# Weight transfers in pairs from expert 8 on in place of expert 10, and the ninth weight buffer for four pieces in place of six

## The chip, the cores and the metric

One core of one Trainium2 chip runs the whole kernel. The metric is the time of one execution on the device in microseconds; the median of three runs of the kernel before is 1223.11 us (1222.31 to 1225.02).

## The reference, cut to what matters

One decoder layer on 256 prompt tokens and 64 sample tokens. First come the norm, an input projection, two kinds of recurrent heads (HGRN2 and RWKV-7) and an output projection. Then comes a mixture of 32 experts, and each token goes to 4 of them. Nothing of the change touches the first part.

```
logits = h @ w_router + b_router
top_val, top_idx = lax.top_k(logits, TOP_K)            # 4 of 32
gates = softmax(top_val)
# for each expert e and its tokens x:
gu = x @ w_gate_up[e] + b_gate_up[e]                   # (n, 1024) @ (1024, 2048)
gate, up = min(gu[:, :D_FF], 7), clip(gu[:, D_FF:], -7, 7)
y  = ((up + 1) * gate * sigmoid(1.702 * gate)) @ w_down[e] + b_down[e]   # (n, 1024) @ (1024, 1024)
out = x_resid + sum over the 4 experts of gate * y
```

All is 32-bit floating point. An expert has 8 MB of gate and up weights and 4 MB of down weights, 12 MB together and 384 MB for all 32.

## The kernel before, in words

The weights of the experts are cut into pieces of 2 MB (128 partitions of 16 KB, `PIECE` = 4096 elements). `weight_pieces` lists them in order of transfer as `PIECES`: the four up pieces of expert 0, then for every expert e from 1 the four up pieces of e and the two down pieces of e - 1, and the last two down pieces. There are 192. The index of a piece in this list is called k here: the up pieces of expert e are k = 6e - 2 to 6e + 1, and the down pieces of expert e are k = 6e + 8 and 6e + 9 (190 and 191 for expert 31).

A piece lives in one of nine places in SBUF. Places 0 to 7 (`wslot`) are taken in turn; place 8, the ninth, is the tile `spare_slot` and is used by the pieces in `ONCE` alone. `piece_slots` works out for each piece its place (`SLOT`) and the piece that was in that place before (`HELD`). A piece may be sent only when TensorE is done with the piece that its place held: `load_piece` (L647) waits for the semaphore `w_used`, which TensorE raises by one after the last matmul on each piece, and then issues the transfer through the helper `load` (L578) on the queue of SyncE. SyncE does this in order of k for all pieces from `FIRST` = 9 on (L687), so a piece whose place is not free holds up all pieces behind it. Nothing else goes through SyncE's queue in this stage, except for one small load at expert 29.

Pieces in `WIDE` are sent in pairs: places 0/1, 2/3, 4/5 and 6/7 lie side by side in SBUF (`wpair`), and one transfer of 4 MB (128 partitions of 32 KB) fills both. It waits for the piece that the second of the two places held, `HELD[k + 1]`. `WIDE` begins at the up pieces of expert 10, k = 58, and ends before those of expert 30, k = 178. From expert `EW` = 8 on the up weights are laid out in rows so that two pieces lie side by side in DRAM too.

TensorE takes the pieces in the same order. `arrived` (L1573) waits until the transfer of a piece has landed. An expert is 8 chunks of up matmuls (`up_chunk`, L1585, two chunks a piece), then the first down piece of the expert before (`down_part`, L1619), eight transposes of this expert's gate and up rows (L1610), and the second down piece. Among the up chunks stand the gather of the tokens of a later expert (L1560), and in every second expert the turning of the slots (L1647) and the scatter of finished rows into the output (L1656). VectorE and ScalarE compute the gated product and add the scattered rows.

Of the kernel before, what the change touches and what calls it, by code (L numbers as in the profile page):

```python
# [38 lines left out]
NE, TOPK, DFF = 32, 4, 1024  # L39
# [211 lines left out]
PIECES = weight_pieces()  # L251
PLACE = {x: k for k, x in enumerate(PIECES)}
EW = 8
WIDE = range(PLACE["up", EW + 2, 0], PLACE["up", NE - 2, 0])


ONCE = (8, 17, 26, 35, 44, 53)
FIRST = 9


def piece_slots():

    slot, before, had, n = [], [], {}, 0
    for k in range(len(PIECES)):
        if k in ONCE:
            s = NWS
# [12 lines left out]
def piece_counts():  # L279

    out, n = [], [0] * (NWS + 1)
    for k in range(len(PIECES)):
        s = SLOT[k]
        if k in WIDE and k % 2:
            out.append(out[-1])
# [25 lines left out]
def build(nc, A, O):  # L311
    ctx = ExitStack()
    with ctx:
# [5 lines left out]
        def S(name):  # L319

            if name not in sems:
                sems[name] = ctx.enter_context(nc.semaphore(name))
            return sems[name]
# [76 lines left out]
        def U(stage, k):  # L400

            return DONE[stage, k - 1]
# [173 lines left out]
        def _(sync):  # L576
# [70 lines left out]
            def load_piece(k):  # L647

                kind, e, j = PIECES[k]
                if k in WIDE:  # L650
                    if k % 2 == 0:
                        sync.wait_ge(S("w_used"), HELD[k + 1] + 1)
                        load(wpair[SLOT[k] // 2], rows_in(kind, e, j, 2), f"w{SLOT[k]}_in")
                    return
                slot_ = wslot[SLOT[k]]
                if k == FIRST:
                    for x in range(2):
                        sync.wait_ge(S("unit_filled"), len(UNITS) + 1 + x)
                        load(slot_[:, 1024 * x:1024 * x + 1024], rows_in(kind, e, j)[:, 1024 * x:1024 * x + 1024], ("w0_in", "mid_in")[x])
                    sync.wait_ge(S("w_used"), 1)  # L660
                    load(slot_[:, 2048:PIECE], rows_in(kind, e, j)[:, 2048:PIECE], "end_in")
                    return
                if HELD[k] is not None:
                    sync.wait_ge(S("w_used"), HELD[k] + 1)
                if k >= len(PIECES) - 4:
                    load(slot_[:, 0:PIECE // 2], rows_in(kind, e, j)[:, 0:PIECE // 2], f"w{SLOT[k]}_in")
                    load(slot_[:, PIECE // 2:PIECE], rows_in(kind, e, j)[:, PIECE // 2:PIECE], ("mid_in", "end_in")[j] if e == NE - 1 else ("x0_wo0_in", "x1_wo1_in")[j])
                else:
                    load(slot_, rows_in(kind, e, j), f"w{SLOT[k]}_in")
# [5 lines left out]
            sync.wait_ge(S("unit_filled"), U("var", 3))  # L675
            load_piece(ONCE[0])
            sync.wait_ge(S("mix_rw"), 3)
# [2384 lines left out]
```

## Time and profile before

| | before |
|---|---|
| median of 3 runs | 1223.11 us (1222.31 to 1225.02) |
| the profiled execution | 1221.51 us, of which the span is 1219.4 us |
| PE (matmul) busy | 1192.9 us (98% of the span) |
| VectorE busy | 447.1 us (37%) |
| ScalarE busy | 259.9 us (21%) |
| read from HBM | 430.01 MB |
| chain of the end, by engine | PE 84%, DMA 14%, VectorE 1% |

The span is the time from the first to the last record of the execution; the time of the runs holds some 2 us beside it. PE's clock was granted in full (0.997 of 2.4 GHz on the mean). The experts' stage runs from about 297 us to the end. Each slice of the page's second part is 1219.4 / 40 = 30.5 us long. SPq is SyncE's queue, on which the transfers are issued. A landing is the moment at which the semaphore of a transfer has its full count, and the page's sixth part and the DMA view give the median of the times from issue to landing.

### The profile page before, as it was taken

What the parts mean: (1) busy time and instruction counts of PE and PEld (TensorE: products, weight loads), DVE (VectorE), ACT (ScalarE), POOL (GpSimd) and SP (SyncE); (2) the same over time, 40 slices, a digit from 0 to 9 for tenths busy, and PEclk for the clock granted to TensorE, in tenths of its full rate; (3) what the DMA queues carried; (4) which work ended last, traced back from release to release, by engine and by line L of the source; (5) the groups of instructions that cost most, each with busy time, mean ns of one, the idle gap of its engine ahead of it and who ended that gap; (6) DMA issues with size and microseconds to landing.
All of it is one profiled execution on the core that took longest, in us unless ns stands there. A gap on an engine that the chain in (4) does not pass through costs nothing.

```text
span 1219.4 us, 18273 instructions
## 1 busy us (share of the span) xinstructions
PE 1192.9 (98%) x7824; PEld 575.6 (47%) x7824; DVE 447.1 (37%) x966; ACT 259.9 (21%) x636; POOL 42.8 (4%) x101
## 2 busy tenths in 40 slices
PE   8999999999999999999999999999999999999996
PEld 6777777745443444444443444444443434443332
DVE  3367766754323332333232232323322323222324
ACT  3114434522220211111120112111111111111213
POOL 8000110100000000000000000000000000000000
PEclk9999999999999999999999999999999999999998
DMA  9732202498999999999999999999999999999996
GB/s 286 180 105 70 79 4 72 141 394 331 426 428 427 405 428 429 427 432 426 430 430 429 431 429 430 431 433 431 430 429 431 430 429 429 432 433 426 425 423 225
DMA packets 48940, 436.11 MB, mean 358 GB/s; under 512 B 11461, under 2 KB 26888, under 8 KB 31450
## 3 DMA queue, kind: packets, MB, share of 16 engines
q1 hardware_dynamic: 47812, 431.87, 85.7%
q0 software_dynamic: 960, 3.02, 0.8%
q8 instruction: 64, 1.05, 0.4%
q14 instruction: 18, 0.15, 0.0%
q10 hardware_dynamic: 86, 0.02, 0.0%
HBM read 430.01 MB, written 4.89 MB: 357 GB/s over the span
## 4 chain that ended last, share of the span: by engine, by line
PE 84%; DMA 14%; DVE 1%; ACT 0%; issue 0%; SPq 0%; DVEq 0%; ACTq 0%
PE bank L1585 30%; PE bank L1619 15%; PE bank L890 10%; DMA ring<-in_w_gate_up 9%; PE bank L1560 7%; PE bank L1656 4%; PE bank L1357 3%; DMA ring<-in_w_down 3%; PE bank L1610 2%; DMA mix<-in_w_gate_up 2%; PE bank L1647 1%; PE bank L1109 1%; PE bank L877 1%; PE bank L923 1%; PE bank L1086 1%; DMA hx<-in_state_shift 0%
## 5 line engine op out<-in xcount | busy, mean ns | idle before, releaser
L1585 PE MATMUL bank<-ring,mix 128*64 128x512 f32 x1504 | 344.0, 598 | 5.3 <-DMA ring<-in_w_gate_up 5.2
L1585 PEld LDWEIGHTS bank<-ring,mix 128*64 128x64 f32 x1504 | 101.6, 136 | 204.1 <-issue 198.2
L1619 PE MATMUL bank<-ring,mix 128*64 128x512 f32 x736 | 168.2, 598 | 0.9 <-DMA ring<-in_w_down 0.8
L2903 DVE TENSOR_TENSOR hTb<-bank,w2a 128x512 f32<-128x512 f32 x32 | 22.1, 691 | 368.5 <-PE bank L1610 368.5
L890 PE MATMUL bank<-hTb,ring 128*128 128x328 f32 (+1 forms) x416 | 121.9, 443 | 1.0 <-DVE hTb L2357 0.4
L2153 ACT ACTIVATE mix<-bank,nf 128x256 f32<-128x256 f32 x64 | 26.8, 470 | 449.4 <-PE bank L1560 449.4
L1585 PE MATMUL bank<-mix 128*64 128x512 f32 x496 | 111.4, 595 | 2.8 <-DMA mix<-in_w_gate_up 2.7
L2956 DVE TENSOR_TENSOR mix<-mix,bank 128x512 f32<-128x512 f32 x70 | 48.2, 689 | 158.4 <-PE bank L1656 158.4
L890 PEld LDWEIGHTS bank<-hTb,ring 128*128 128x128 f32 x416 | 76.4, 190 | 33.9 <-issue 2.3
L1619 PEld LDWEIGHTS bank<-ring,mix 128*64 128x64 f32 x736 | 49.6, 136 | 90.0 <-issue 84.0
L1585 PEld LDWEIGHTS bank<-mix 128*64 128x64 f32 x496 | 35.3, 137 | 72.0 <-issue 69.7
L1560 PE MATMUL bank<-mix,hx 128*128 128x256 f32 x240 | 66.1, 418 | 0.0
L2924 DVE SCALAR_TENSOR_TENSOR y_low<-bank,gc,y_high 64x512 fp32r<-64x512 f32 x62 | 46.5, 750 | 49.6 <-ACT y_high L2228 49.1
L1560 PEld LDWEIGHTS bank<-mix,hx 128*128 128x128 f32 x240 | 55.5, 300 | 9.1 <-issue 8.4
L2228 ACT ACTIVATE y_high<-bank,gc 64x512 fp32r<-64x512 f32 x62 | 42.3, 682 | 76.1 <-DVE gc L2938 40.2
L1619 PE MATMUL bank<-mix 128*64 128x512 f32 x240 | 54.8, 598 | 0.0
L1656 PEld LDWEIGHTS bank<-y_high,slot_rows 128*128 128x128 f32 (+1 forms) x96 | 16.2, 186 | 62.5 <-issue 62.5
L2218 ACT ACTIVATE bank<-hTb 128x512 f32<-128x512 f32 x32 | 19.2, 601 | 111.5 <-DVE hTb L2905 111.5
L1656 PE MATMUL bank<-y_high,slot_rows 128*128 128x512 f32 (+1 forms) x96 | 42.3, 480 | 0.0
L2207 ACT COPY g2w<-bank 128x512 f32<-128x512 f32 x32 | 18.7, 585 | 90.8 <-PE bank L1585 90.8
L1560 PEld LDWEIGHTS bank<-raw,hx 64*128 64x128 f32 x112 | 26.9, 303 | 22.9 <-issue 22.7
L1357 PE MATMUL bank<-ring,mix 128*128 128x512 f32 (+1 forms) x96 | 36.9, 600 | 0.0
(445 smaller groups left out, 1132.7 us busy)
## 6 DMA issues: line engine op xcount, KB each, us to landing
ring<-in_w_gate_up SPq DMA_DIRECT2D x30, 4096.0 KB, 24.9
ring<-in_w_gate_up SPq DMA_DIRECT2D x34, 2048.0 KB, 16.1
ring<-in_w_down SPq DMA_DIRECT2D x15, 4096.0 KB, 27.6
mix<-in_w_gate_up SPq DMA_DIRECT2D x10, 4096.0 KB, 25.2
ring<-in_w_down SPq DMA_DIRECT2D x13, 2048.0 KB, 16.3
mix<-in_w_gate_up SPq DMA_DIRECT2D x11, 2048.0 KB, 15.3
mix<-in_w_down SPq DMA_DIRECT2D x5, 4096.0 KB, 28.3
ring<-in_w_in SPq DMA_DIRECT2D x14, 1024.0 KB, 5.6
```

Source lines behind the costliest of these rows:

```text
L890: last_ = mm(b_[:, 0:nn], slot(chunk)[:, c, P * k:P * k + P], hT[:, c, 0:nn], start=(c == 0), stop=(c == KT - 1))
L1357: last_ = mm(o_, lhs_, wo[c_ // 4][:, c_ % 4, 512 * h_:512 * h_ + 512], start=(c_ == 0), stop=(c_ == KT - 1))
L1560: last_ = mm(o, rows_of(tile_, c, r), sel[tile_][0:TN[tile_], :], start=(first and tile_ == TORD[0]), stop=(tile_ == TORD[2]), skip_group_ ...
L1585: last_ = mm(b_[64 * half:64 * half + 64, :].rearrange("s (p q) -> s p q", q=4), toks, cols[:, half], start=(c == 0), stop=(c == KT - 1))
L1610: last_ = nc.tensor.transpose(b_[:, P * q:P * q + P], src[:, q:NCOL:4], ident[:, :])
L1619: last_ = mm(b_[r:r + 64, :], lhs, w[:, o:o + NCOL], start=(j == 0 and q == 0), stop=(j == 1 and q == 3))
L1656: last_ = mm(o[:, :], scatr[r[g], g, P * tile_:P * tile_ + P], y_[r[g], g, :], start=(y_ is yhir and g == half), stop=(stop and y_ is ylor ...
L2153: ins = a(xg[n // 4 % 2][:, 256 * c:256 * c + 256], b[:, 256 * x:256 * x + 256], ACT.Copy, scale=nf2[int(n // 4 >= EW // 4)][:, c:c + 1])
L2228: ins = a(yhir[r, k, :], banks[2][r, :], ACT.Copy, scale=gc[r, g:g + 1])
L2903: v.tensor_tensor(halves(gg), halves(banks[3][:, :]), bias(e, 0), ALU.add).then_inc(S("g1"), 1)
L2924: ins = v.scalar_tensor_tensor(out=ylor[r, k, :], in0=banks[2][r, :], scalar=gc[r, g:g + 1], in1=yhif[r, k, :], op0=ALU.mult, op1=ALU.subt ...
L2956: ins = v.tensor_tensor(o, o, b[:, :], ALU.add)
```

## The change

Two constants change. `WIDE` begins at the up pieces of expert `EW` = 8, k = 46, in place of `EW` + 2 = 10, k = 58. `ONCE` loses its last two pieces, 44 and 53. Pieces 44 and 53 then take places 0 and 1 of the rotation, and the places of all pieces from 44 on move: by one step for 44 to 52 and by two from 53 on.

```
-WIDE = range(PLACE["up", EW + 2, 0], PLACE["up", NE - 2, 0])
-ONCE = (8, 17, 26, 35, 44, 53)
+WIDE = range(PLACE["up", EW, 0], PLACE["up", NE - 2, 0])
+ONCE = (8, 17, 26, 35)
```

The piece of which TensorE must be done before k is sent, worked out by `piece_slots` and `load_piece`:

| k | 44 | 45 | 46 | 47 | 48 | 49 | 50 | 51 | 52 | 53 | 54 | 55 | 56 | 57 | 58/59 | 60/61 | 62/63 | 64/65 |
|---|---|---|---|---|---|---|---|---|---|---|---|---|---|---|---|---|---|---|
| before | 35 | 36 | 37 | 38 | 39 | 40 | 41 | 42 | 43 | 44 | 45 | 46 | 47 | 48 | 50 | 52 | 55 | 57 |
| after | 36 | 37 | 39 (46/47) | | 41 (48/49) | | 43 (50/51) | | 45 (52/53) | | 47 (54/55) | | 49 (56/57) | | 51 | 53 | 55 | 57 |

## Rows read from the trace of the kernel before

**Rows 1.** The page's second part: GB/s moved by the DMA engines in 40 slices.

```profile
GB/s 286 180 105 70 79 4 72 141 394 331 426 428 427 405 428 429 427 432 426 430 430 429 431 429 430 431 433 431 430 429 431 430 429 429 432 433 426 425 423 225
```

**Rows 2.** PE's waits, 889 to 1219 us: waited for, total us, times, longest.

```profile
PE bank L1585 <- DMA ring<-in_w_gate_up: 5.2, 7, 1.3
PE bank L1585 <- DMA mix<-in_w_gate_up: 2.7, 3, 1.3
...
PE bank L1619 <- DMA ring<-in_w_down: 0.8, 2, 0.4
```

**Rows 3.** The chain of the end, in order: start, us, step.

```profile
477.80 3.58 PE bank L1619 x16
...
703.40 3.58 PE bank L1619 x16
...
865.93 24.42 DMA ring<-in_w_gate_up
...
1165.12 33.98 DMA ring<-in_w_down
```

**Rows 4.** Windows: length, busy us by engine, PE clock, DMA share, GB/s.

```profile
411.00:500.00 89.00, 89.00 (x398) 35.88 (x400) 25.39 (x54) 12.92 (x30) 0.00 (x0) 1.00 1.01 428
...
575.00:580.00 5.00, 5.00 (x26) 1.72 (x24) 1.50 (x2) 0.28 (x1) 0.00 (x0) 1.00 0.87 374
...
600.00:1100.00 500.00, 494.11 (x2180) 208.70 (x2178) 145.57 (x321) 79.28 (x203) 0.00 (x0) 1.00 1.00 431
```

**Rows 5.** SyncE's timeline: start, us, transfer issued (k = 45, 46, 48/49, 50, 52, 54, 56, 62, 64).

```profile
471.01 0.33 SPq L578 DMA_DIRECT2D ring<-in_w_down  x1
474.44 0.33 SPq L578 DMA_DIRECT2D ring<-in_w_gate_up  x1
...
486.17 3.77 SPq L578 DMA_DIRECT2D ring<-in_w_gate_up  x2
...
494.32 0.33 SPq L578 DMA_DIRECT2D ring<-in_w_down  x1
...
504.44 0.33 SPq L578 DMA_DIRECT2D mix<-in_w_gate_up  x1
...
517.11 0.33 SPq L578 DMA_DIRECT2D ring<-in_w_gate_up  x1
...
527.53 0.33 SPq L578 DMA_DIRECT2D ring<-in_w_down  x1
...
560.84 0.33 SPq L578 DMA_DIRECT2D ring<-in_w_down  x1
...
573.51 0.33 SPq L578 DMA_DIRECT2D ring<-in_w_gate_up  x1
```

**Rows 6.** PE's timeline: start, us, matmuls merged (k = 47-49, 51, 53, 66).

```profile
525.55 8.80 PE L1585 MATMUL bank<-ring,mix 128*64 128x512 f32 x40
...
538.88 3.65 PE L1619 MATMUL bank<-mix 128*64 128x512 f32 x16
...
548.74 1.94 PE L1585 MATMUL bank<-spare_slot,mix 128*64 128x512 f32 x8
...
607.67 0.65 PE L1585 MATMUL bank<-ring,mix 128*64 128x512 f32 x2
```

**Rows 7.** DMA view, issues at 399.97, 404.71, 471.01, 560.84, 573.51 us, b_down's: KB, us to landing.

```profile
ring<-in_w_gate_up SPq DMA_DIRECT2D x1, 2048.0 KB, 8.7
...
ring<-in_w_gate_up SPq DMA_DIRECT2D x1, 2048.0 KB, 9.4
...
ring<-in_w_down SPq DMA_DIRECT2D x1, 2048.0 KB, 17.6
...
ring<-in_w_down SPq DMA_DIRECT2D x1, 4096.0 KB, 15.7
...
ring<-in_w_gate_up SPq DMA_DIRECT2D x1, 4096.0 KB, 13.4
...
hx<-in_b_down SPq DMA_DIRECT2D x1, 128.0 KB, 2.2
```

## Prediction

> **What bounds the kernel now.** I read the slices of the whole span first. From about 305 us to 1180 us two things are full at once: PE is busy nine tenths and more (the PE line of the same table), and the DMA engines move 425 to 433 GB/s in nearly every slice [rows 1]. So I asked which of the two is late. The waits of PE say it: that view of 270 to 830 us, and of 600 to 889 us, has no row with a transfer; from 889 us to the end it waits 8.7 us for them (5.2 + 2.7 + 0.8, in twelve waits) [rows 2]. The chain of the end agrees: its long DMA links begin at 865.93 us, and the last, ending in the final experts' down weights, lasts 33.98 us, up to 1199.1 us; behind it stand only the last matmuls, the scatter, the norm and the output [rows 3].
>
> The reason lies in two rates. PE alone needs 56.4 us for two experts: the first down matmul of an expert starts at 477.80 us, and that of the expert eight later at 703.40 us, so (703.40 - 477.80) / 4 = 56.4 [rows 3]. Two experts are 12 pieces of 2 MB, 25.17 MB, and at 431 GB/s [rows 4] they need 58.4 us. PE gains 2 us per two experts on the transfers; early on it lives on what lies ready in the buffers, and when that is used up it runs at the pace of the transfers. From there every microsecond that the stream of transfers has lost anywhere is a microsecond at the end. The question is thus only: how late does the stream run behind expert 11, where both versions have the same waits again?
>
> **What the change does to the sum.** I count pieces k in order of transfer; the up pieces of expert e are k = 6e-2 to 6e+1, then come the two down pieces of expert e-1. Up to k = 43 nothing changes. Then three things do.
>
> (1) Pieces 46 to 57 go as six transfers of 4 MB in place of twelve of 2 MB. The SyncE queue gets six DMA instructions and six waits less, of 0.33 us each [rows 5]; that queue waits for buffers most of the time, so this is worth nothing. The rate rises from 428 to 431 GB/s [rows 4]: two pieces take 9.80 us as two transfers and 9.73 us as one. Gain 6 x 0.07 = 0.4 us.
>
> (2) A pair can be issued only when both of its places are free, so it waits for its second place.
>
> (3) Pieces 44 and 53 don't use the ninth buffer any more. So, by (2) and (3), every piece or pair from 44 to 61 waits for PE to be done with a piece one or two later than before (the table of the change has them). (The waits of k = 62 and up are the same before and after: 55, 57, 59 and so on.)
>
> (2) and (3) cost nothing as long as the queue of transfers holds enough. To see whether it does, the time at which PE releases each piece is read from the issues of before, because SyncE issues a piece right when its place is released: piece 36 was released at 471.01 (issue of 45), 37 at 474.44 (of 46), 39 at 486.17 (issue of 48), 41 at 494.32 (50), 43 at 504.44 (52), 45 at 517.11 (54), 47 at 527.53 (56), 55 at 560.84 (62), 57 at 573.51 (64) [rows 5]. The others come from the matmuls that end: 49 at 534.2 (after 525.55 + 8.80), 51 at 542.4 (538.88 + 3.65), 53 at 550.6 (548.74 + 1.94) [rows 6].
>
> Next, how late may an issue be? The one 4 MB transfer of before that met a nearly empty queue is k = 64. It was issued at 573.51 and landed 13.4 us later, at 586.9, while its predecessor, issued at 560.84, landed 15.7 us later, at 576.5 [rows 7]: 10.4 us apart in place of 9.73, so the stream lost 0.7 us. The windows show the hole: 374 GB/s from 575 to 580 us where the mean is 431 [rows 4]. So I take: landing = the later of (previous landing + 9.73) and (issue + 13.4). An issue must come 3.7 us ahead of the previous landing. Two 2 MB transfers that met a short queue (issued at 399.97 and 404.71 us) took 8.7 and 9.4 us [rows 7] where the data alone take 4.9: 3.8 and 4.5 us, near the same.
>
> The steps, from piece 45, which landed at 471.01 + 17.6 = 488.6 [rows 7]. Pieces 44 and 45 are issued 3.4 us later than before and still land on time: 474.44 + 8.7 = 483.1 is ahead of 488.6. Then:
> 46/47: issue 486.17, so 499.6 and not 498.3 (1.3 lost);
> 48/49: issue 494.32, lands 509.3; 50/51: issue 504.44, lands 519.0 (nothing lost);
> 52/53: issue 517.11, so 530.5 and not 528.8 (1.7 lost);
> 54/55: issue 527.53, so 540.9 and not 540.2 (0.7 lost);
> 56/57: 534.2, lands 550.7; 58/59: 542.4, lands 560.4; 60/61: 550.6, lands 570.1; 62/63: 560.84, lands 579.8;
> 64/65: issue 573.51, lands 589.6: the hole of before is gone, since the previous transfer now ends later.
> Before, 64/65 landed at 586.9. The stream is 2.7 us late there: lost 3.7, won back 0.4 by the rate and 0.7 at the old hole (the rest is rounding).
>
> Is PE held up earlier, which would move the releases that I used? No: PE reads 49 only in the 8.80 us behind 525.55 [rows 6], so 46 to 48 not much ahead of that, and they land at 499.6 and 509.3; the smallest reserve near the change is that of 66, which PE reads at 607.67 us [rows 6], and which landed at 586.9 + 9.7 = 596.6 before and lands at 599.3 now. So PE runs as before for a while, with 2.7 us less in store, and meets the pace of the transfers one to two pairs of experts sooner (2.7 / 2 = 1.3). Behind that all is shifted by 2.7 us. At the very end nothing swallows it, since PE waits for the last down weights until 1199.1 us [rows 3] and then has only its own work and the rest of them.
>
> **Sum.** Profiled execution: span 1219.4 us, 1221.51 us with what lies around it. Plus 2.7 gives 1224.2 for that execution. The median of the runs is 1.6 us above it, 1223.11; so the forecast is 1223.11 + 2.7 = 1225.8 us.
>
> **The page and the row.** What the trace shows is 13.4 us from issue to landing with an almost empty queue [rows 7]. The Trainium skill, DMA: Bandwidth & Descriptors, "Anatomy of one DMA", gives a fixed cost of about 2.0 us and a time of 2.0 us + bytes / 436 GB/s, fitted on GpSimd's path; for 4 MB that is an estimate of 11.6 us. By it the needed lead is 1.9 us, and only 52/53 would be late. The row differs by 1.8 us, and I go by the row; the other result is rival B. The same page's rules advise coalescing many small transfers into one large one, which would speak for the change; here the rate rows of both sizes stand at 428 and 431 GB/s, so that is worth 0.4 us.
>
> **The rivals.**
> A, the forecast: +2.7 us, 1225.8.
> B, not slower: the stream loses less than k = 64's landing suggests. The 128 KB load of the down bias, which has 0.3 us of data, landed 2.2 us after its issue [rows 7], so an issue costs as little as 1.9 us beside its data. With landing = issue + 9.73 + 1.9 = issue + 11.6, 52/53 lands at 528.7 and not 527.5, 54/55 at 539.1 and 64/65 at 587.8: +0.9 us, 1224.0. If even that doesn't occur (engines that finish at different times take up the last microsecond), the change keeps only the better rate and the closed hole: -0.4 - 0.7 = -1.1 us, 1222.0. It decides at a lead of 1.9 us in place of 3.7. For it speaks that k = 64 had a lead of 3.0 us (576.5 - 573.51) and yet the DMA share only fell to 0.87 for 5 us [rows 4]; against it stand the two 2 MB loads with 3.8 and 4.5 us.
> C, more: the overhead of the 9.4 us landing (4.5 us) holds for pairs too: issue + 14.2. Then 46/47 lands at 500.4, 52/53 at 531.3, 54/55 at 541.7, and 64/65 at 590.4: +3.5 us, 1226.6.
> D, PE hides it: if the end were set by PE, the result would be 0, 1223.1. Against it stand the DMA waits from 889 us on and the last link of the chain [rows 2, 3].
> E, the shorter queue starves the stream again and again behind expert 11. Against it: the same waits as before hold there, and a stream that is later makes the queue fuller at each issue.
>
> **How the numbers follow.** Chances: A 0.45, B 0.25 (0.9 and -1.1 about alike), C 0.17, D 0.08, E 0.05. A measurement of this kernel tells about 0.2% from no change, 2.45 us. A's 2.7 us stands right at that mark: I give it 0.27 slower and 0.18 same. C and E count as slower (0.20 of 0.22), D and nearly all of B as same. Slower 0.48, same 0.47, faster 0.05. The range goes from the closed-hole case with some scatter of a median (1222.4) to C with some scatter (1227.6).
>
> **What would show it.** Right: the two-piece transfers of k = 46, 52 and 54 land about 13.4 us after their issue, with holes in the DMA rate near 488, 519 and 529 us; no hole near 575; PE has no new wait before 600 us; its first DMA wait comes between 770 and 860 us and not at 890; the sum of these waits grows by about 2.7 us from 8.7. Wrong: holes absent (B), pieces landing 14 us or more after issue (C), a PE wait between 480 and 700 us (then releases move too), or DMA landings that are late while the end isn't (D).

## The result and the profile after

The changed kernel takes 1226.22 us (median of 14 runs, 1224.41 to 1228.12), the kernel before 1223.14 us in its 14 runs. The ratio is 1.0024, with a 95% interval of 1.0017 to 1.0031, which is +2.1 to +3.8 us. The forecast was +2.7 us. The profiled execution of the changed kernel took 1225.37 us with a span of 1223.2 us, 0.9 us below its median. Its span is 3.8 us longer than that of the profiled execution of before.

The windows of the changed kernel show where the stream of transfers has holes. The columns are those of [rows 4]; the last two are the DMA share and GB/s.

```profile
485.00:490.00 5.00, 5.00 (x26) 1.65 (x24) 2.48 (x4) 1.36 (x2) 0.00 (x0) 1.00 0.90 324
515.00:520.00 5.00, 5.00 (x26) 1.59 (x23) 3.42 (x9) 1.36 (x2) 0.00 (x0) 1.00 0.72 249
525.00:530.00 5.00, 5.00 (x24) 1.92 (x24) 2.76 (x12) 0.84 (x2) 0.00 (x0) 1.00 1.06 403
575.00:580.00 5.00, 5.00 (x26) 1.72 (x24) 1.50 (x2) 0.39 (x1) 0.00 (x0) 1.00 0.98 419
```

The same three early windows of the kernel before:

```profile
485.00:490.00 5.00, 5.00 (x26) 1.72 (x24) 2.37 (x4) 1.36 (x2) 0.00 (x0) 1.00 1.02 433
515.00:520.00 5.00, 5.00 (x26) 1.68 (x24) 3.42 (x9) 1.36 (x2) 0.00 (x0) 1.00 1.02 436
525.00:530.00 5.00, 5.00 (x25) 1.92 (x26) 2.76 (x12) 0.84 (x2) 0.00 (x0) 1.00 0.99 423
```

Two holes are new, near 488 and near 518 us, with a shallow third at 528 us. The hole of before at 575 to 580 us (374 GB/s in [rows 4]) is gone. PE is busy for the whole of each window in both kernels: the holes have not reached it yet.

SyncE's timeline of the changed kernel gives the issues of these transfers (start, us, transfer; k = 46/47 and 48/49, 50/51, 52/53 and 54/55, 58/59, 62/63, 64/65). Where [rows 5] has the release, the issue stands 0.1 us behind it:

```profile
486.28 8.47 SPq L578 DMA_DIRECT2D ring<-in_w_gate_up  x2
504.55 0.33 SPq L578 DMA_DIRECT2D mix<-in_w_down  x1
517.22 10.75 SPq L578 DMA_DIRECT2D ring<-in_w_gate_up  x2
...
542.68 0.33 SPq L578 DMA_DIRECT2D mix<-in_w_gate_up  x1
...
560.95 0.33 SPq L578 DMA_DIRECT2D ring<-in_w_down  x1
573.62 0.33 SPq L578 DMA_DIRECT2D ring<-in_w_gate_up  x1
```

The DMA view of the changed kernel gives us to landing for those issued at 486.28 (46/47), 517.22 (52/53), 527.64 (54/55), 542.68 (58/59), 560.95 (62/63) and 573.62 us (64/65):

```profile
ring<-in_w_gate_up SPq DMA_DIRECT2D x1, 4096.0 KB, 13.0
...
ring<-in_w_gate_up SPq DMA_DIRECT2D x1, 4096.0 KB, 14.0
...
ring<-in_w_gate_up SPq DMA_DIRECT2D x1, 4096.0 KB, 13.7
...
mix<-in_w_gate_up SPq DMA_DIRECT2D x1, 4096.0 KB, 18.9
...
ring<-in_w_down SPq DMA_DIRECT2D x1, 4096.0 KB, 20.0
...
ring<-in_w_gate_up SPq DMA_DIRECT2D x1, 4096.0 KB, 17.1
```

So the landings are 499.3, 531.2, 541.4, 561.5, 581.0 and 590.7 us (by the trace's unrounded times). The first three and the last stood at 499.6, 530.5, 540.9 and 589.6 in the forecast. 64/65 landed at 586.9 us before [rows 7]: the stream is 3.8 us late there in this execution (0.1 us of it is the later start), and the span grew by as much.

PE's waits over the whole stage, changed kernel (columns as in [rows 2]):

```profile
PE bank L1585 <- DMA ring<-in_w_gate_up: 8.4, 10, 1.3
PE bank L1585 <- DMA mix<-in_w_gate_up: 1.8, 3, 0.6
PE bank L1610 <- ACT us L2208: 1.2, 1, 1.2
PE bank L1619 <- DMA ring<-in_w_down: 1.1, 2, 0.6
...
PE bank L1619 <- DMA mix<-in_w_down: 0.3, 1, 0.3
```

The waits for transfers sum to 11.6 us, where those of [rows 2] sum to 8.7: +2.9. The first DMA link of the chain of the end now begins at 806.08 us and not at 865.93, and the last ends at 1168.11 + 34.69 = 1202.8 us and not at 1199.1 [rows 3]. The chain of the changed kernel (start, us, step):

```profile
806.08 29.13 DMA mix<-in_w_gate_up
...
1168.11 34.69 DMA ring<-in_w_down
```

### The profile page after: what moved, and what is told of

The parts are those of the page before. It is cut to its first block, busy times and chain, and to the rows that moved or that the text cites. A ratio compares the mean times of both kernels' runs of the same rounds, so it can differ in the third digit from the quotient of the medians.

```text
span 1223.2 us, 18267 instructions
## 1 busy us (share of the span) xinstructions
PE 1193.4 (98%) x7824; PEld 575.3 (47%) x7824; DVE 447.0 (37%) x966; ACT 259.9 (21%) x636; POOL 42.8 (4%) x101
## 4 chain that ended last, share of the span: by engine, by line
PE 81%; DMA 17%; DVE 1%; ACT 0%; issue 0%; SPq 0%; DVEq 0%; ACTq 0%
PE bank L1585 29%; PE bank L1619 14%; PE bank L890 10%; DMA mix<-in_w_gate_up 7%; PE bank L1560 7%; DMA ring<-in_w_gate_up 6%; PE bank L1656 4%; PE bank L1357 3%; DMA ring<-in_w_down 3%; PE bank L1610 2%; PE bank L1647 1%; PE bank L1109 1%; PE bank L877 1%; PE bank L923 1%; PE bank L1086 0%; DMA hx<-in_state_shift 0%
## 5 line engine op out<-in xcount | busy, mean ns | idle before, releaser
L1585 PE MATMUL bank<-ring,mix 128*64 128x512 f32 x1504 | 341.7, 597 | 8.6 <-DMA ring<-in_w_gate_up 8.4
L1585 PEld LDWEIGHTS bank<-ring,mix 128*64 128x64 f32 x1504 | 103.7, 137 | 211.6 <-issue 205.1
L1619 PE MATMUL bank<-ring,mix 128*64 128x512 f32 x768 | 175.8, 599 | 1.1 <-DMA ring<-in_w_down 1.1
L1619 PEld LDWEIGHTS bank<-ring,mix 128*64 128x64 f32 x768 | 50.9, 136 | 91.7 <-issue 83.4
```

What stands on the lines that cost most here:

```text
L1585: last_ = mm(b_[64 * half:64 * half + 64, :].rearrange("s (p q) -> s p q", q=4), toks, cols[:, half], start=(c == 0), stop=(c == KT - 1))
L1619: last_ = mm(b_[r:r + 64, :], lhs, w[:, o:o + NCOL], start=(j == 0 and q == 0), stop=(j == 1 and q == 3))
```

## The experiments

Each kernel ran in five rounds beside the kernel before. Changes in us below are the ratio to before, times 1223. One more number serves throughout: the time from issue to landing of 64/65. PE releases its place at the same point of its own work in every kernel, so what exceeds 13.4 us (before) is how late the stream is there, whatever that execution's start was like. It holds some lateness that no edit made: piece 40, which is issued ahead of every edit, took 16.1 us from issue to landing in the execution of before, 17.0 in that of the changed kernel and 16.1 to 17.0 in the others. A hole wipes this out; where there is none, up to 0.9 us of a lateness can be of that kind.

**The ninth buffer alone.**

```
-WIDE = range(PLACE["up", EW, 0], ...)        # the changed kernel
+WIDE = range(PLACE["up", EW + 2, 0], ...)
```

> Only the ninth buffer's part of the change: four pieces use it, the pairs still begin at expert 10. Theory (the loss comes from pairs that are issued less than about 3.7 us ahead of the previous landing): pieces 44 to 61 are issued one release later than before, but each still 5 us or more ahead of the previous landing, so no hole is added; k = 64 lands at 587 us as before and the time is that of before, +0.0 us (within 0.7). Rival (the loss comes from the shallower ninth buffer): most of the +3 us is there, +2 to +3.

Measured: 1.0003 (0.9994 to 1.0012), +0.3 us. The transfer 64/65 of this kernel, issued at 573.60 us, and the windows where the changed kernel has its holes:

```profile
ring<-in_w_gate_up SPq DMA_DIRECT2D x1, 4096.0 KB, 13.7
```

```profile
485.00:490.00 5.00, 5.00 (x26) 1.66 (x24) 2.46 (x4) 1.36 (x2) 0.00 (x0) 1.00 0.99 423
515.00:520.00 5.00, 5.00 (x27) 1.58 (x23) 3.42 (x9) 1.36 (x2) 0.00 (x0) 1.00 0.99 423
```

No hole, and 13.7 us. This half of the edit costs nothing that the runs can tell (-0.7 to +1.5 us): with single pieces the queue has room for one release less.

**Pairs from expert 9 on.**

```
-WIDE = range(PLACE["up", EW, 0], ...)
+WIDE = range(PLACE["up", EW + 1, 0], ...)
```

> Ninth buffer for four pieces, pairs from expert 9 (k = 52) and not 8. Theory: the issue of 52/53 at 517 us (release of 45) is what sets the lateness, whatever 46 to 51 did, so it lands about 13.4 to 14 us later at 530.5 to 531, 54/55 at 541, and k = 64 lands as late as in the full change: +2.6 to +3.6 us. Rival (each of the six pairs costs its share): half of the full change, +1.5 us.

Measured: 1.0017 (1.0008 to 1.0026), +2.1 us (1.0 to 3.2). 52/53 landed 12.4 us after its issue at 516.69, so at 529.1, sooner than expected; 54/55 landed 13.9 us after 527.11, at 541.0, as expected. 64/65 took 18.1 us, which is 4.7 us late and more than expected; 58/59 landed in this execution 11.3 us behind its predecessor though it was issued early. The median lies below the expected +2.6 to +3.6 us and about midway between the theory and the rival's +1.5; its interval holds both, so this run alone doesn't decide.

**The first pair alone.**

```
-WIDE = range(PLACE["up", EW, 0], ...)
+WIDE = (46, 47, *range(PLACE["up", EW + 2, 0], PLACE["up", NE - 2, 0]))
```

> Ninth buffer for four pieces, 46/47 as a pair, 48 to 57 one by one, pairs again from expert 10. Theory: 46/47 is issued at 486.2 us, lands at 499.3 to 499.9 where 498.3 would be in time: 1.1 to 1.6 us are lost, 0.7 of it is won back at k = 64, where before had a hole: +0.5 to +0.9 us. Rival (a pair costs a fixed share, 3 us / 6): +0.5. Rival (any loss shows in full at the end): +1.3.

Measured: 1.0007 (0.9998 to 1.0016), +0.9 us; 64/65 took 14.2 us, 0.8 us late. That is within the theory's 0.5 to 0.9, but the time can't tell it from the rivals' 0.5 and 1.3. The trace doesn't show the way that was expected: 46/47, issued at 488.37 us, took 12.9 us and landed 9.7 us behind its predecessor, so it lost nothing itself; the pieces behind it lost 0.7 us between them, and piece 40 had been 0.7 us late already.

**Three of the six pairs.** The three that the forecast's steps called in time are kept, and the three that they called late are sent as single pieces.

```
-WIDE = range(PLACE["up", EW, 0], ...)
+WIDE = (*range(48, 52), *range(56, PLACE["up", NE - 2, 0]))
```

> The changed kernel with three of its six new pairs (48/49, 50/51, 56/57) kept and the other three (46/47, 52/53, 54/55) sent one by one. Theory (only a pair issued too close to the previous landing costs): 48/49 and 50/51 are issued in time or nearly (lost 0 to 0.4 us), 56/57 loses about 0.6 us, and the hole of before at k = 64 takes nearly all of it back: k = 64 lands at 587 to 587.7 us, +0.0 to +0.8 us against before, within noise of it. Rival (each pair costs a share): half of the changed kernel, +1.5.

> The changed kernel once more, on the same chip as the three pairs. +3 us against before (+2.6 by the sum of the steps, up to +3.8 by its first trace); k = 64 lands at 590 to 591 us where its issue is at 573.6.

Measured in the same comparison: three pairs 1.0006 (0.9997 to 1.0015), +0.7 us; the changed kernel 1.0026 (1.0016 to 1.0036), +3.2 us. Three kept pairs cost 0.7 us (-0.4 to +1.8), and adding 46/47, 52/53 and 54/55 brings the other 2.5 (the two intervals just fail to meet, 1.0015 and 1.0016): a pair has no price of its own that shows, its place in time has. In the traces 64/65 took (three pairs, issued at 575.41, then the changed kernel, issued at 574.87):

```profile
ring<-in_w_gate_up SPq DMA_DIRECT2D x1, 4096.0 KB, 15.7
```

```profile
ring<-in_w_gate_up SPq DMA_DIRECT2D x1, 4096.0 KB, 16.3
```

The first is a miss: 13.5 to 14.2 had been expected. 62/63 landed at 562.74 + 17.4 = 580.1, from which 64/65 would have taken 14.4 us; it landed at 591.1, 11.0 us behind 62/63. A single trace thus carries 1 us and more of such scatter, and between these two kernels the medians of the runs decide and not the traces. In the second execution of the changed kernel 46/47, 52/53 and 54/55 took 13.3, 14.4 and 13.7 us from issue to landing.

**One more release to wait for.** If late issues are the cause, then later ones must cost what the same rule gives.

```
-sync.wait_ge(S("w_used"), HELD[k + 1] + 1)
+sync.wait_ge(S("w_used"), HELD[k + 1] + (2 if k < 58 else 1))
```

> The changed kernel, with each of its six new pairs waiting for one more piece of TensorE than it needs. Theory: issues at the releases of 40, 42, 44, 46, 48, 50 in place of 39, 41, 43, 45, 47, 49, that is at 490, 499, 512, 521, 531, 538 us; by landing = later of (previous + 9.72) and (issue + 13.4) k = 64 lands 6.9 us later than before, with TensorE's smallest reserve still 3 us, so the time is +7 us (6.5 to 8), some 4 us more than the changed kernel. Rival (TensorE sets the end and hides late transfers): no more than the changed kernel, +3. Rival (the queue of transfers is starved by anything that waits): over +10.

Measured: 1.0055 (1.0041 to 1.0069), +6.7 us (5.0 to 8.4). 64/65 took 20.4 us, 7.0 us more than before where the rule gave 6.9. The windows show the holes that were made, the first of them with less than half of the DMA engines' time in use, and PE busy throughout:

```profile
488.00:494.00 6.00, 6.00 (x28) 2.17 (x26) 1.62 (x3) 0.90 (x2) 0.00 (x0) 1.00 0.45 145
500.00:506.00 6.00, 6.00 (x25) 1.88 (x22) 2.35 (x8) 0.00 (x0) 0.00 (x0) 1.00 1.00 385
511.00:517.00 6.00, 6.00 (x34) 2.50 (x32) 2.54 (x5) 2.11 (x10) 0.00 (x0) 1.00 0.75 273
```

This rules out that PE hides late transfers: 64/65 was 7 us late at 575 us, PE had no wait for any transfer before 600 us, and the end came 6.7 us later 650 us on.

**Pairs only from expert 12 on, and none at all.** Both with the six pieces in the ninth buffer, as before.

```
-ONCE = (8, 17, 26, 35)
+ONCE = (8, 17, 26, 35, 44, 53)
-WIDE = range(PLACE["up", EW, 0], ...)
+WIDE = range(PLACE["up", EW + 4, 0], ...)    # the other kernel: range(0)
```

> The kernel before (ninth buffer for six pieces) with pairs only from expert 12 (k = 70) on: 58 to 69 go one by one, each issued at its own release. Theory: the hole that before has at k = 64 (0.7 us) closes, since 64 and 65 are issued apart and earlier (555 to 574 us), against 6 x 0.07 = 0.4 us of lost rate: 0.1 to 0.6 us faster, no difference that the runs can tell; the trace has no window under 400 GB/s between 560 and 600 us. Rival (pairs themselves are what costs): 1 us or more faster.

> The kernel before with no pairs at all: all pieces go as 2 MB transfers. Theory: only the rate differs, 9.79 us for two pieces in place of 9.72, on 60 pairs, less the closed hole at k = 64: 60 x 0.07 - 0.7 = +3.5 us (3 to 4.5). Rival (a transfer costs nothing extra, large or small): -0.7. Rival (a fixed cost of 2 us for each transfer that is not hidden): over +100 us.

Measured: from expert 12, 1.0003 (0.9994 to 1.0013), no difference; none, 1.0042 (1.0028 to 1.0055), +5.1 us (3.4 to 6.7). The first kernel's trace has no hole between 560 and 600 us (421 to 433 GB/s), so it closes the hole of before; the expected gain of 0.1 to 0.6 us doesn't show, but lies within the interval (-0.7 to +1.6 us). The kernel with no pairs lies above the expected 3 to 4.5 us, though its interval holds them, so the pairs seem to bring more than I had put. The window of the kernel with no pairs, against 431 in [rows 4]:

```profile
600.00:1100.00 500.00, 494.00 (x2180) 207.26 (x2178) 145.63 (x322) 80.29 (x204) 0.00 (x0) 1.00 1.01 427
```

At 427 GB/s two pieces take 9.82 us, 0.09 more than at 431 and not 0.07 (the windows are rounded to 1 GB/s, which is some 0.02 us here). 60 pairs make 5.4 us, less the 0.7 of the hole 4.7, near the measured 5.1. On the six pairs of the expert 12 kernel it is 0.5 us against 0.7 won.

## Why the prediction was right, step by step

**What bounds the kernel: right.** The end follows the stream of transfers one to one, within about 1 us for a single execution. The second column is the time from issue to landing of 64/65 less 13.4 us, the third the span less the issue of 64/65, against 1219.4 - 573.51 = 645.9 us before; the last compares the runs.

| kernel | late at 64/65 | end later | runs |
|---|---|---|---|
| changed | 3.7 | 3.7 | +2.9 |
| changed, second execution | 2.9 | 3.5 | +3.2 |
| one more release | 7.0 | 7.5 | +6.7 |
| pairs from expert 9 | 4.7 | 3.7 | +2.1 |
| three pairs | 2.3 | 1.4 | +0.7 |
| first pair alone | 0.8 | 1.5 | +0.9 |
| ninth buffer alone | 0.3 | 1.0 | +0.3 |

PE's waits for transfers grew from 8.7 to 11.6 us, and began between 770 and 860 us, as forecast.

**(1), the rate: right in sign, a little small.** 0.09 us a pair and not 0.07: 0.5 us for the six. The gain on the six pairs was not measured by itself.

**(2) and (3), the later releases: right together.** The forecast's list of which transfers come late (46/47, 52/53, 54/55) is that of the holes, and with these three sent singly 2.5 of 3.2 us are gone. The forecast treated (2) and (3) together, and the cost is that of both: each of the three pairs waits for a piece two later than before (39 and not 37, 45 and not 43, 47 and not 45), one step by the pairing and one by the ninth buffer. The run of the ninth buffer alone shows that (3) by itself costs nothing measurable. The pairing alone was not run, and these kernels can't have it: with piece 44 in the ninth buffer piece 46 takes place 1, and the pairs begin at even places. Its releases stand in the trace of before, though. The pairs would wait for pieces 38, 44 and 46, which were released at the issues of 47, 53 and 55:

```profile
481.43 0.33 SPq L578 DMA_DIRECT2D ring<-in_w_gate_up  x1
...
512.36 0.33 SPq L578 DMA_DIRECT2D spare_slot<-in_w_gate_up  x1
...
520.54 0.33 SPq L578 DMA_DIRECT2D ring<-in_w_gate_up  x1
```

That is 4.7, 4.8 and 7.0 us ahead of the releases of 39, 45 and 47, and by the forecast's rule all three would land in time. So, as an estimate, neither half of the edit makes a hole by itself; the two together do.

**Issue + 13.4 us: near on the mean, not a constant.** In the two traces of the changed kernel 52/53 took 14.0 and 14.4 us, 54/55 took 13.7 in both, and 46/47 took 13.0 and 13.3; with pairs from expert 9, 52/53 took 12.4 and 54/55 13.9. With 14.0 for 52/53 and 13.7 for 54/55 the stream is some 0.3 us later than forecast.

**The sum: the total held, the term for 46/47 did not matter.** The forecast lets 46/47 lose 1.3 us. In the profiled execution it was issued 3.3 us ahead of the previous landing and lost nothing, although the rate fell to 324 GB/s: piece 45, issued at 474.55 us, landed at 489.6 and not 488.6, and 46/47 followed 9.7 us behind it. Most of that 1 us was there ahead of the change, since piece 40 was 0.8 us late already; it is scatter between executions. In the second execution 46/47 was issued 2.5 us ahead and lost 1.1 us. Neither changes the end, because the landing of 52/53 is set by its own issue and not by what came before. A hole wipes out the lateness that the stream brings along: with pairs from expert 9 nothing was lost ahead of 52/53, and 54/55 still took 13.9 us. In the sum the losses before such a hole don't add up. What counts is the last transfer that is late by its own issue: 54/55 in the first execution of the changed kernel, and 52/53 in the second, where 54/55 landed 9.7 us behind it.

**The rest of this execution's 3.8 us.** 2.7 was forecast, 0.1 is the later start, and 0.3 is in the landing of 54/55. Then 58/59, issued 8.4 us ahead of its predecessor's landing, landed 0.7 us late. With pairs from expert 9 the same transfer lost 1.5 us, in the second execution of the changed kernel nothing, and such slips of 0.3 to 1.6 us stand behind 600 us in every trace, that of before too. It is scatter that differs between executions: the medians lie 3.1 us apart. What makes it stays open. The queue that loads instructions moved a packet in this stretch, but it moved one in the same stretch of before as well (556 to 572 us), where 58/59 landed in time.

**Slips in the forecast's working.** The ends of the matmuls in [rows 6] are 534.35, 542.53 and 550.68 us and not 534.2, 542.4 and 550.6; these three transfers are not late by their issue, so nothing follows. By the estimate of 11.6 us not only 52/53 would be late: rival B's own numbers have 54/55 at 539.1 us, 0.7 us late. The chances as given add up to 0.47 for slower and 0.48 for same, not the other way round.

**The rivals.** B (a needed lead of 1.9 us, +0.9 us) is out: the interval begins at +2.1 and the holes are there. By the Trainium skill, DMA: Bandwidth & Descriptors, "Anatomy of one DMA", whose fit is of GpSimd's path, 4 MB would be an estimate of 11.6 us. The traces don't agree: no 4 MB transfer here that met a hole took less than 12.1 us, and the longest took 14.9. C (+3.5 us) can't be told from A by the runs; in the traces 54/55 lies between the two, and 52/53 from 12.4 to 14.4. D (PE hides it) is ruled out by the kernel with one more release, E by the windows behind 600 us, 430 GB/s where before had 431:

```profile
600.00:1100.00 500.00, 491.26 (x2164) 207.18 (x2161) 145.52 (x321) 78.55 (x201) 0.00 (x0) 1.00 1.00 430
```

No variant was faster than the kernel before. The only hole of before in this stretch is worth 0.7 us, and closing it by single pieces costs, by 0.09 us a pair, about as much in rate.

## What to carry to other kernels

When a stream of transfers is the bound but the engine that eats it is a little faster, the lateness of the last landing that a hole has moved shows in full at the end, even if nobody waits for hundreds of microseconds after it; look for holes in short windows of the DMA rate and then at how far apart the landings are, not in the waits. A dip of the rate alone is not a loss, as 46/47 showed. Fusing two transfers makes the first half wait for the place of the second, so before fusing, hold each issue against the landing of its predecessor: in the eight traces with 4 MB transfers up to 64/65, all seven that were issued less than 2.5 us ahead lost 1.1 to 4.5 us, those with 3.0 to 4.0 us lost 0 to 1.2, and those with more lost 0.3 at most, but for three that lost 0.7 to 1.5 us. The fused transfer itself brought 0.09 us. Fuse where the queue is already deep.

## What the runs showed of the hardware that was not expected

The time from issue to landing of a 4 MB transfer into a queue that ran dry is not constant. In the kernel with one more release to wait for, those issued at 490.97, 500.74, 513.72 and 521.90 us took:

```profile
ring<-in_w_gate_up SPq DMA_DIRECT2D x1, 4096.0 KB, 13.5
...
ring<-in_w_gate_up SPq DMA_DIRECT2D x1, 4096.0 KB, 13.3
...
mix<-in_w_down SPq DMA_DIRECT2D x1, 4096.0 KB, 12.1
...
ring<-in_w_gate_up SPq DMA_DIRECT2D x1, 4096.0 KB, 14.9
```

With 9.73 us of data that is 2.4 to 5.2 us beside it. The second met no hole (it landed 9.6 us behind the first); the third and fourth did, by 2.0 and 1.2 us, and lie at the two ends. What makes the difference stays open.

The starting point of the experts' stage varies between executions by up to 2.6 us: 64/65 was issued at 573.1 to 575.7 us in kernels whose work up to there is the same for PE, and at 573.6 and 574.9 us in the two executions of the changed kernel. How much of the scatter of the runs (1221.66 to 1225.02 us before) this makes is not shown, since each kernel but the changed one has one trace. It is a reason to read lateness from issue to landing and not from the time since the start.
